# More tokens routed through indirect DMAs, fewer through one-hot products: 160 and 24 groups in place of 128 and 32

## The reference

```
q   = (t @ w_q) as (token, 8 heads, 2 halves, 128)
sc  = q . sub_keys                      # 128 scores for each half
top 16 of each half, their 16 x 16 sums, top 16 of these -> idx (of 16384 experts), g = softmax(best)
act = gelu(u_tab[idx] . t)              # one number for each token and choice
out = sum over 8 heads and 16 choices of g * act * v_tab[idx]
```

## Time and profile before

| what | value |
| --- | --- |
| median of 3 runs | 1643.32 us (1642.72 to 1643.47) |
| the profiled execution's own time | 1644.13 us |
| its span, from the first to the last instruction | 1642.0 us |
| TensorE busy | 1623.3 us (99%) |
| VectorE busy | 1263.3 us (77%) |
| ScalarE busy | 906.6 us (55%) |
| GpSimd busy | 286.9 us (17%) |
| mean granted TensorE clock | 0.999 of full speed |

### The profile page before, as it was taken

How to read it: one execution, slowest core, us unless ns; L and a number is a source line. 1 busy time by engine, 2 the same in 40 slices (tenths; PEclk the granted TensorE clock), 3 DMA queues, 4 the chain that set the end, 5 groups by cost and what they waited for, 6 DMA issues and landing times.

```text
span 1642.0 us, 30006 instructions
## 1 busy us (share of the span) xinstructions
PE 1623.3 (99%) x10571; PEld 1467.2 (89%) x10571; DVE 1263.3 (77%) x2390; ACT 906.6 (55%) x1527; POOL 286.9 (17%) x175
## 2 busy tenths in 40 slices
PE   9999999999999999999999999999999999999998
PEld 8999899999999999888888887988888888788886
DVE  7888877987967788766666667778777877587777
ACT  5766645555555555555555555665555545555554
POOL 1000003887788730000000000010000000000000
PEclk9999999999999999999999999999999999999999
DMA  7767666777777764777777786445666644356663
GB/s 236 237 234 233 227 202 181 181 178 170 180 174 149 167 154 142 230 219 216 217 217 216 217 253 200 161 144 175 190 187 190 206 153 147 112 188 186 189 188 108
DMA packets 123782, 310.01 MB, mean 189 GB/s; under 512 B 32432, under 2 KB 50608, under 8 KB 123312
## 3 DMA queue, kind: packets, MB, share of 16 engines
q1 hardware_dynamic: 101232, 294.94, 58.5%
q0 software_dynamic: 20736, 8.46, 4.4%
q10 hardware_dynamic: 1728, 5.45, 1.0%
HBM read 297.72 MB, written 10.55 MB: 188 GB/s over the span
## 4 chain that ended last, share of the span: by engine, by line
PE 86%; issue 7%; DVE 4%; ACT 1%; DMA 1%; POOL 0%; SPq 0%; POOLq 0%; DVEq 0%; ACTq 0%
PE ps L1219 13%; PE ps L1221 13%; PE ps L1220 13%; PE ps L1269 10%; PE ps L1271 10%; PE ps L1273 10%; PE ps L1239 9%; PE ps L1241 5%; PE ps L1386 2%; PE ps L1252 1%; DVE low L1693 1%; DVE held_low L1693 0%; DVE arena L1762 0%; PE ps L1360 0%; DMA raw<-in_w_mix 0%
## 5 line engine op out<-in xcount | busy, mean ns | idle before, releaser
L1693 DVE TENSOR_TENSOR low<-raw,high 128x1024 fp32r<-128x1024 f32 (+1 forms) x516 | 621.6, 1210 | 132.6 <-ACT high L820 131.3
L820 ACT ACTIVATE high<-raw 128x1024 fp32r<-128x1024 f32 (+1 forms) x517 | 538.3, 1044 | 251.5 <-PE ps L1221 183.4
L1219 PE MATMUL ps<-x_parts,low 128*128 128x256 f32 x1840 | 525.1, 285 | 0.9 <-DVE x_parts L1809 0.9
L1221 PE MATMUL ps<-x_parts,high 128*128 128x256 f32 x1840 | 520.6, 283 | 0.0
L1220 PE MATMUL ps<-x_parts,high 128*128 128x256 f32 x1840 | 520.5, 283 | 0.0
L1219 PEld LDWEIGHTS ps<-x_parts,low 128*128 128x128 f32 x1840 | 352.9, 192 | 2.7 <-issue 1.2
L1220 PEld LDWEIGHTS ps<-x_parts,high 128*128 128x128 f32 x1840 | 353.0, 192 | 0.0
L1221 PEld LDWEIGHTS ps<-x_parts,high 128*128 128x128 f32 x1840 | 352.8, 192 | 0.0
L767 POOL DMA_INDIRECT routed<-h_tok,subln x128 | 254.8, 1991 | 133.4 <-DVE h_tok L2074 66.9
L1239 PE MATMUL ps<-x_parts,high 128*128 128x512 f32 x672 | 238.8, 398 | 0.0
L1269 PE MATMUL ps<-high,yl 128*128 128x512 f32 x640 | 197.7, 390 | 0.0
(11 more groups left out here) (356 smaller groups left out, 1727.6 us busy)
## 6 DMA issues: line engine op xcount, KB each, us to landing
raw<-in_u_tab SPq DMA_DIRECT2D x128, 512.0 KB, 3.7
raw<-in_v_tab SPq DMA_DIRECT2D x128, 512.0 KB, 4.3
raw<-in_ffn_in SPq DMA_DIRECT2D x88, 512.0 KB, 4.2
raw<-in_w_mix SPq DMA_DIRECT2D x56, 512.0 KB, 4.5
raw<-in_ffn_out SPq DMA_DIRECT2D x44, 512.0 KB, 3.6
routed<-arena POOLq DMA_DIRECT2D x16, 512.0 KB, 4.1
raw<-in_w_query SPq DMA_DIRECT2D x16, 512.0 KB, 4.2
raw<-in_diff_qk SPq DMA_DIRECT2D x16, 512.0 KB, 3.7
```

The lines of the kernel that those rows point to most:

```text
L820: a.activation(w_high(p, 0, n), cols(raw, p, 0, n), ACT.Copy).then_inc(slot_high[p.slot], 1)
L1219: pe.matmul(dst, left[1], right[0], start=start, stop=False)
L1221: return pe.matmul(dst, left[0], right[0], start=False, stop=stop)
L1693: v.tensor_tensor(w_low(p, 0, n), cols(raw, p, 0, n), w_high(p, 0, n).bitcast(F32), ALU.subtract).then_inc(slot_low[p.slot], 1)
```

## The change

The first 160 tokens go through `routed`, whose rows grow from 128 to 160 entries, and 24 groups are left for the 96 others. The 32 tokens that are added (the first of the second tile) have 128 choices each. They are repacked: VectorE copies weight and index to `by_spread`, a DMA writes the 32 partitions to HBM, another reads them back as 128 partitions, 32 tokens by 4 choices. Each of 32 more indirect DMAs then adds 4 choices of 32 tokens. In GpSimd's queue they stand in eights behind and between the halves of heads 5, 6 and 7, in two parts of four for each, and the last eight at the end. The clears become 20. In SyncE's queue both repacking DMAs stand between loads of the inner stage, and the waits for the groups and for all scatters stand in step 0 of the outer stage. The products of a group are walked with the four tokens innermost, in `arena` (adjacent there) and in PSUM (512 bytes apart there); before, a token's keys were innermost.

```diff
+EXTRA = 32
+SPREAD = PARTS // EXTRA
+OF_HEAD = 16 // SPREAD
+ROUTED = PARTS + EXTRA
+GROUPS = (SEQ - ROUTED) // 4
-ZERO_PARTS = 16
+ZERO_PARTS = 20
...
-            return min(GROUPS, max(0, (p - LEAD + 1) * GROUPS // (PAIRS - LEAD)))
+            return min(GROUPS, max(0, (p - LEAD + 1) * GROUPS // (PAIRS - LEAD - 1)))
...
-            return bank(g % 4).rearrange("p (t j) -> p t j", t=4)
+            return bank(g % 4).rearrange("p (t j) -> p j t", t=4)
...
-            return arena[:, :].rearrange("p (j t) -> p j t", t=SEQ)[:, j:j_end, t:t + 4].rearrange("p j t -> p t j")
+            return arena[:, :].rearrange("p (j t) -> p j t", t=SEQ)[:, j:j_end, t:t + 4]
...
+        routed_part = [h_tok[:, 512 * n:512 * n + ROUTED] for n in range(4)]
...
             for k in range(EARLY, NKEYS):
+                if k == EARLY + 10:
+                    sp.wait_ge(chosen_ready, ROUNDS)
+                    for a in range(2):
+                        sp.dma_start(by_place[a], by_spread[a][0:EXTRA]).then_inc(packed_out, 16)
+                if k == EARLY + 12:
+                    sp.wait_ge(packed_out, 32)
+                    sp.dma_start(params[:, 32:32 + 2 * EXTRA], repacked).then_inc(packed_in, 16)
                 load(piece_u(k), u_tab[k])
...
                 if j == 0:
                     sp.wait_ge(sel_turned, 1)
+                    sp.wait_ge(group_done, GROUPS)
                     sp.wait_ge(scattered, 16 * SLOTS)
-                if j == 2:
-                    sp.wait_ge(group_done, GROUPS)
+                    sp.wait_ge(scattered_extra, 16 * EXTRA)
...
+            for n in range(2 * KC, ZERO_PARTS):
+                pool.dma_start(cleared[n], zeros).then_inc(zeroed, 16)
...
+            def scatter(h, first, last):
+                if first == 0 and h >= 1:
+                    pool.wait_ge(scattered, 16 * 16 * h)
+                for n in range(16 * h + first, 16 * h + last):
+                    pool.indirect_dma_start(...).then_inc(scattered, 16)
+            def scatter_extra(h):
+                if h >= 1:
+                    pool.wait_ge(scattered_extra, 16 * OF_HEAD * h)
+                for n in range(OF_HEAD * h, OF_HEAD * (h + 1)):
+                    pool.indirect_dma_start(...).then_inc(scattered_extra, 16)
             for h in range(HEADS):
                 if h % 2 == 0:
                     pool.wait_ge(chosen_ready, h // 2 + 1)
+                if h < 5:
+                    scatter(h, 0, 16)
+                    continue
+                if h == 5:
+                    pool.wait_ge(packed_in, 16)
+                scatter_extra(2 * (h - 5))
+                scatter(h, 0, 8)
+                scatter_extra(2 * (h - 5) + 1)
+                scatter(h, 8, 16)
+            scatter_extra(6)
+            scatter_extra(7)
...
+                chain.step(v.tensor_scalar(first_place[:, 32:64], slot_i[:, 1, heads], float(ROUTED), token_extra, ALU.mult, ALU.add))
...
+                v.scalar_tensor_tensor(out=extra_index[:, of_round], in0=slot_j[:, 1, heads].rearrange("p (n q) -> p n q", q=SPREAD),
...
+                v.tensor_copy(extra_weight[:, of_round], slot_weight[:, 1, heads].rearrange("p (n q) -> p n q", q=SPREAD)).then_inc(chosen_ready, 1)
...
-                a = at(arena, it * (4 * SEQ) + j * SEQ, PARTS)
+                a = at(arena, it * (4 * SEQ) + j * SEQ, ROUTED)
...
                     one_hots(0)
+                    v.wait_ge(packed_out, 32)
                     one_hots(1)
```

More of the change, by code:

```diff
@@ L239, in sem @@
             return ctx.enter_context(nc.semaphore(name))
-        routed = nc.dram_tensor("routed", (NKEYS, PARTS, PARTS), F32, kind="Internal").ap()
+        routed = nc.dram_tensor("routed", (NKEYS, PARTS, ROUTED), F32, kind="Internal").ap()
+        repacked = nc.dram_tensor("repacked", (PARTS, 2 * EXTRA), F32, kind="Internal").ap()
         raw = sb("raw", [PARTS, RING * D])
@@ L390, in build @@
         weight = spare[:, 0:PARTS]
-        minus_weight = params[:, 0:GROUPS]
-        routed_part = [h_tok[:, 0:PARTS], subln[:, :], h_tok[:, PARTS:2 * PARTS], h_tok[:, 2 * PARTS:3 * PARTS]]
+        minus_weight = params[:, 0:PARTS // 4]
+        routed_part = [h_tok[:, 512 * n:512 * n + ROUTED] for n in range(4)]
+        by_spread = [h_tok[:, (8 + a) * PARTS:(9 + a) * PARTS].rearrange("p (q n) -> p q n", q=SPREAD) for a in range(2)]
+        extra_weight, extra_index = (t.rearrange("p q n -> p n q") for t in (by_spread[0], by_spread[1].bitcast(U32)))
+        packed_weight = params[:, 32:32 + EXTRA]
+        packed_index = params[:, 32 + EXTRA:32 + 2 * EXTRA].bitcast(U32)
         zeros = part(17408, D)
@@ L430, in build @@
         best = part(tk + 7744, 64)
-        first_place = part(tk + 7808, 32)
-        expsum = part(tk + 7840, 32)
+        first_place = part(tk + 7808, 64)
+        expsum = part(tk + 7872, 32)
         v_tok = part(0, TB * D)
@@ L468, in build @@
         mix2 = stats[:, 52:54]
-        token = stats[:, 44:45]
+        token, token_extra = stats[:, 44:45], stats[:, 45:46]
         sign, subln_column = stats[:, 54:55], stats[:, 55:56]
@@ L487, in build @@
         scattered, sel_turned, sel_ready = sem("scattered"), sem("sel_turned"), sem("sel_ready")
+        scattered_extra, packed_out, packed_in = sem("scattered_extra"), sem("packed_out"), sem("packed_in")
         one_hots_ready, act_hots_ready, distance_ready = (sem(n) for n in ("one_hots_ready", "act_hots_ready", "distance_ready"))
@@ L638, in _ @@
                     load(piece_u(k), u_tab[k])
+            by_place = repacked.rearrange("(q t) (a n) -> a t q n", t=EXTRA, a=2)
             for k in range(EARLY, NKEYS):
+                if k == EARLY + 10:
[5 more added lines that the diff above has]
+                    sp.dma_start(params[:, 32:32 + 2 * EXTRA], repacked).then_inc(packed_in, 16)
                 load(piece_u(k), u_tab[k])
@@ L2065, in _ @@
                 chain.wait()
-                chain.step(v.tensor_scalar(first_place, slot_i[:, 0, heads], float(PARTS), token, ALU.mult, ALU.add))
+                chain.step(v.tensor_scalar(first_place[:, 0:32], slot_i[:, 0, heads], float(ROUTED), token, ALU.mult, ALU.add))
+                chain.step(v.tensor_scalar(first_place[:, 32:64], slot_i[:, 1, heads], float(ROUTED), token_extra, ALU.mult, ALU.add))
                 v.wait_ge(exp_ready, it + 1)
@@ L2070, in _ @@
                 link(v.reciprocal(sums, sums))
-                v.scalar_tensor_tensor(out=slot_index[:, heads], in0=slot_j[:, 0, heads], scalar=float(PARTS * PARTS), in1=first_place,
+                v.scalar_tensor_tensor(out=slot_index[:, heads], in0=slot_j[:, 0, heads], scalar=float(PARTS * ROUTED),
+                                       in1=first_place[:, 0:32], op0=ALU.mult, op1=ALU.add)
+                of_round = slice(2 * OF_HEAD * it, 2 * OF_HEAD * (it + 1))
+                v.scalar_tensor_tensor(out=extra_index[:, of_round], in0=slot_j[:, 1, heads].rearrange("p (n q) -> p n q", q=SPREAD),
+                                       scalar=float(PARTS * ROUTED), in1=first_place[:, 32:64].rearrange("p (n q) -> p n q", q=SPREAD),
                                        op0=ALU.mult, op1=ALU.add)
@@ L2074, in _ @@
                     ins = v.tensor_tensor(weights4[:, b], weights4[:, b], sums[:, 2 * b:2 * b + 2].unsqueeze(2).to_broadcast([PARTS, 2, 16]), ALU.mult)
-                ins.then_inc(chosen_ready, 1)
+                chain.step(ins)
+                chain.wait()
+                v.tensor_copy(extra_weight[:, of_round], slot_weight[:, 1, heads].rearrange("p (n q) -> p n q", q=SPREAD)).then_inc(chosen_ready, 1)
                 ahead(u[15])
```

12 lines of the change are left out of this document (8 added, 4 removed).

## The result

The change makes the kernel slower: 1659.86 us (median of 6 runs, 1655.65 to 1662.32) against 1643.75 us (6 runs on the same chip, 1642.72 to 1646.34). The ratio is 1.0094, with a 95% interval of 1.0084 to 1.0103. The forecast was 1655.3, in a range of 1645 to 1663. The profiled execution took 1657.26, its span is 1655.5; against the 1644.13 of the profiled execution before that is 13.1 us more, where the sum said 12.1. It is the second fastest of the six runs: by medians the change costs 16.1 us, where the forecast had 12.0. Most lines have moved by 10 to 54: 767 is now 787 (a head's scatters) and 795 (the extra ones), 666 is 684, 609 is 619, 1693 is 1736, 820 is 863, 1269 is 1312 and 2123 is 2175.

The account below looks back on a forecast made before the run. TensorE, busy 99% of the span, was taken to bound the kernel. An outer stage 9.4 us later plus 2.7 of clock gave 12.1 on 1644.13; on the median, 1643.32 + 12.0 = 1655.3, range 1645 to 1663 (8 in 10).

Parts of the forecast that it names:

- The gain from the groups: TensorE's inner stage: 32 groups become 24, 8 x 0.89 = 7.1 us less, so the outer stage could start at 652.4.
- The walk: VectorE's group product: price between 2.45 and 1.04 ns per element, near the lower; hidden by VectorE, so worth nothing.
- The queue: GpSimd's 80 remaining indirect DMAs: completion T at about 659.6, needed by 643.1; gain turns to loss at 650.2.
- issue beyond 0.30: GpSimd's queue: issue gaps above 0.30 us hold 9.0 us over 128 DMAs, so 5.6 for 80.
- free run at the end: GpSimd's queue: with VectorE standing still at the end, eight DMAs run unhindered, 2.2 us less.
- The chain behind T: From the last scatter's completion to TensorE's outer stage: piece 1's issue, landing and splitting, then VectorE's work, 9.25 us.
- The clock: TensorE's outer stage: after 16 us idle the clock may be at 1.2 GHz; bounds 0 and 5.8, taken 2.7 us.
- The clears: Four more 512 KB clears behind the last mixer round, mostly in idle DMA windows: bounds 0 and 2, taken 0.7 us.
- A: Rival on GpSimd's queue: the scatter is in time at 1.95 us or less per DMA, giving 1636.9; chance 0.16.
- B: Rival on GpSimd's queue: the scatter is later still at 2.29 us per DMA, 14 us more, 1669; chance 0.07.
- C: Rival at TensorE's outer stage: the scatter is late but the clock holds, 1652.6; chance 0.17.
- D: Rival: VectorE bounds the inner stage if PSUM's wide step is very dear; 34 us, 1678; chance 0.03.

Follow-up runs that it names:

- the clears late: The change with its four added clears issued during the first choosing round, not in a burst behind the last mixer round: 1653.64 us, ratio 1.0068.
- the best version: The clears late, plus repacking round by round and loads of v pieces 1 to 3 ahead of the scatter waits: 1638.44 us, ratio 0.9969.
- the one by rounds: The clears late, with the 32 tokens' choices repacked round by round and four extra DMAs behind each head: 1644.60 us, ratio 1.0005.
- two experiments: Four clears of an unused tensor added to the kernel before, 1648.97 us (+5.3); and the clears late, 1653.64 us (6.1 less than the change).
- the walk alone: The kernel before, with its 32 groups, and only the new walk of the products (tokens innermost): 1643.73 us, ratio 0.9999.
- the loads already first: The clears late, with the loads of v pieces 1 to 3 ahead of SyncE's waits for the scatters: 1648.33 us, ratio 1.0024.
- the kernel with the clock kept up: The clears late, with 50 unread products between TensorE's inner and outer stage: 1649.30 us, ratio 1.0034.

## Why the prediction was right

**The gain from the groups: right.** 7.1 us were forecast. The kernel with the clears late ends its inner stage at the forecast 652.4, and the best version starts its outer stage at 652.73. In the changed kernel the inner stage ended at 657.4, the 5.0 us of the clears later.

**The walk: right**, and shown alone. The product came to the lower of the two prices (1.03 ns per element), and the time did not move.

**The queue: right in kind; its end to 0.1 us is luck, by terms that cancel.** T, the completion of the last scatter, was forecast at 659.6 and came at 659.5.

| term | forecast | measured |
| --- | --- | --- |
| start of the last 80 | 481.8 | 484.6 |
| 80 preparings and their issue | 168.8 | 148.0 + 23.8 = 171.8 |
| waits left | 2.8 | 1.7 |
| issue beyond 0.30 | 5.6 | 0 |
| free run at the end | -2.2 | in the 171.8 |
| end of the last to T | 2.8 | 1.4 |

The clears (below) put the start 2.8 us late, and the DMAs took 5.2 us more than forecast if the free run at the end is counted with them (171.8 against 166.6). Against that the gaps of issue that were expected from the earlier trace rows were absent (5.6), and both waits were shorter (1.1 and 1.4). In the clears-late kernel, which has neither the burst nor its delay, T came at 654.6. That is still above the 650.2 at which the case turns, so the sign didn't hang on the cancelling.

The reason given for the dear DMAs was right in kind and unsharp: not each meeting with a two-input instruction costs. The DMA of 482.08, which the prediction takes for one that met none, had a low part begin inside it:

```profile
482.33 1.23 DVE L1693 TENSOR_TENSOR low<-raw,high 128x1024 fp32r<-128x1024 f32 x1
```

It took 1.54 us all the same. A DMA is slow if it begins inside such an instruction, as the count of the 80 shows.

**The chain behind T: 1.0 us too short, and by another path.** 9.25 us forecast; 10.3 measured in the change, 9.5 in the clears-late kernel and in the one by rounds. The forecast went over the landing of piece 1 and then VectorE's work in a row. Measured, VectorE was through with piece 1 and its two weighings and stood still for 1.49 us, because the last to come was piece 2: issued 1.6 us after T and not 0.45, landed after 5.92 and not 4.3 (the median over all `v` loads), in a row of loads and blocks released together. In return piece 1's low part and the weighings (1.8) don't count.

**The clock: right, its size by luck.** 2.7 us were forecast, chosen near the middle of bounds of 0 and 5.8. Measured: the first six pairs of products take 675.27 - 669.78 = 5.5 us, at the pace behind them 6 x 0.46 = 2.8, so 2.7; and 2.6 between the two kernels that differ in the products that keep the clock up.

The Trainium skill (TensorE: Matmul & The Clock Gate, What's actually happening) says that the clock is gated down by idleness and released by sustained activity. These runs agree: 0.50 behind waits of 12.4, 11.7, 4.8 and 2.75 us, and 1.00 from 645 to 675 us in the run that put products into the wait.

**The clears: the step that was mis-sized.** "Bounds 0 and 2 us, taken 0.7": two experiments say 5.3 and 6.1, outside the bounds. The step reasoned from an idle window at 200 us. But the clears go out at 192, beside the query weights, and these landed after 9.4 us and not 3.5; and there is a second charge, the clock at 0.50 behind TensorE's wait, that the bounds didn't hold. The delay passes on to GpSimd's queue, whose first scatter came 5.5 us later than before and not 1.3, and through it to the outer stage. In the profiled execution this was masked by the missing issue gaps and the shorter waits. By medians, where the forecast is 4.6 us too low, it is the one term of that size; that it accounts for the 4.6 is argued and not shown, since the queue's end varies between executions.

**The rivals.** A (in time) is refuted for this kernel; its 1636.9 is nearly what the best version reaches (1638.4), by taking the waits out of GpSimd's queue and the loads from behind the scatters. B did not occur: 2.15 us for each DMA against 2.29. C is refuted by the clock of 0.50. D is refuted by the walk alone. (D's sum leaves out the gain of the groups: with it, its 1678 would be 1670.)

So the loss of 16.1 us by medians is made of the 32 DMAs' queue, less what the groups give (10.0, with the clears late), and of the clears (6.1); the order of loads in SyncE's queue (5.3) and the repacking at once instead of by rounds (10.3 with the loads already first: 1648.33 to 1638.44, each against its own chip's kernel before) are how far each is avoidable.

## What to carry to other kernels

A serial queue with slack is a resource like an engine: when work is moved to it, add up its whole length, and where its completion gates a stage, put the loads that don't depend on it ahead of the wait. An idle stretch of the DMA engines doesn't make a transfer free; ask what is in flight when it is issued, and who waits for that. A wait of a few microseconds on TensorE can cost more than its length: here the clock fell behind waits of 2.75 to 12.4 us, and behind the one of 11.7 that cost 2.6 us more.

## What the runs showed of the hardware

- The granted clock fell to 0.50 after a wait of only 2.75 us at 205 us in the changed kernel, and after 4.8 us in the kernel by rounds. It was back at its upper level after 4 to 6 us of work (208.2 to 214.4, 669.8 to 675.3, and 657.3 to 661.8 by rounds).
- A single burst of four 512 KB clears cost 5.3 us, though they landed 4.9 us after their issue (median) and nothing waited for them: the loads beside them landed after 9.4 us and not 3.5.
- Of the last 80 indirect DMAs of the changed kernel those take 1.54 us to prepare that begin outside of the two VectorE instructions with two SBUF inputs (33), 1.82 those that begin inside line 2144 (0.68 us long), and 2.26 those that begin inside a low part (1.23 us long). A low part that begins during the DMA costs it nothing (28 of the 33).
- So GpSimd's DMAs fall into step with VectorE. In the timeline above they take 1.81, 2.38 and 1.54 us, and with three issues of 0.30 the next begins 6.64 us after the first: one pair of the inner stage (6.65). The mean of 1.85 is then set by how the pair's instructions lie; that the step is held by them is argued from the rows, no kernel with other VectorE work was run.
- Most kernels whose outer stage waits for this queue vary more: the change spans 6.7 us over 6 runs, the clears-late kernel 5.0 over 4, the kernel before 2.7 over 23 on the latter's chip. But the kernel with the clock kept up, which waits as well, spans 1.8 over 5, and the one without the extra DMAs 4.1 over 8. What shifts the time from one execution to the next stays open.
- The longer gaps of issue in the kernel before (2 to 4.4 us, three of them) came down to one of 2.9 us in the changed one and to none in the kernels by rounds. Their cause stays open too.
